# A decoder step on one core: the first stage in a new order, and the normalisation's root as a power on GpSimd

## The chip, the cores and the metric

The kernel runs on one core of one Trainium2 chip. The metric is the device time of the whole program in microseconds (us): the median of three runs. One more execution was taken by the hardware profiler. Its span (first to last instruction) and the rows of its trace are what this document argues from. The engines are TensorE (PE in the rows, PEld for its weight loads), VectorE (DVE), ScalarE (ACT), GpSimd (POOL) and SyncE (SP), which here only issues transfers. They run side by side and meet at semaphores.

## What is computed

One inference step of a decoder with two layers, for a prompt of 256 tokens and 8 sample streams of 4 tokens. The kernel holds all T = 288 tokens as columns of a transposed activation `xT` (128 partitions x 8 chunks x 288). Layer 0 mixes tokens by a diagonal complex state space (S5) with a gated linear unit (GLU), layer 1 by three groups of dilated attention. Each is followed by a PEER channel mixer with 16384 single-neuron experts. Every sub-layer normalises its input and shifts and scales it by vectors made from a condition `c`:

```
def rms_norm(x, gain=None):
    y = x32 * lax.rsqrt(jnp.mean(x32 * x32, axis=-1, keepdims=True) + EPS)
def adaln_params(c, w, b):
    return jnp.split(jax.nn.silu(c) @ w + b, 6, axis=-1)
def modulate(x, gain, shift, scale):
    return rms_norm(x, gain) * (1.0 + scale[:, None, :]) + shift[:, None, :]
def s5_mixer(h, h0, ...):
    a_bar = jnp.exp(lam * dt)
    b_bar = ((a_bar - 1.0) / lam)[..., None] * lax.complex(b_re, b_im)
    bu = jnp.einsum('bsgp,gnp->bsgn', u, b_bar)
    _, states = lax.associative_scan(_linear_recurrence_combine, (a, bu), axis=1)
    y = jnp.real(jnp.einsum('bsgn,gpn->bsgp', states, c_mat)) + d_skip * u
    z = y @ w_glu
    out = z[..., :D] * jax.nn.sigmoid(z[..., D:])
```

There are four such normalisations, q = 0 to 3: ahead of S5, of PEER 0, of attention and of PEER 1.

## The kernel before, in words

All large weights come through one stream of 680 tiles of 128 x 1024 fp32 (512 KB each) into a ring of four slots. SyncE issues the load of tile n as soon as TensorE has finished tile n - 4 (`tile_done`). The first 48 tiles are the adaLN weights of layer 0 (`ada0(k)`: `ada_tile`, 4 matrix products on 9 columns, line 1000 of the profile). They form six blocks of eight. ScalarE copies a finished block's rows out (`ada_row`, line 366, four instructions), and TensorE turns them into columns (`ada_turn`, line 1010, eight products) at the fourth tile of a later block. S5's normalised input needs blocks 0 and 1, the GLU's residual block 2, and PEER the rest.

The first stage, up to the GLU's first product (line 1161), works in a written order, with no planner:

- VectorE computes the powers of the transition (`times_a`, lines 1572 to 1576) up to `s5_w`, squares `xT` (`square_x`, line 1522), and reduces three small tables.
- `chunk_weights(q)` on TensorE (line 1049) spreads these powers over four PSUM banks, for q = 0 and 1. `chunk_products(q)` on VectorE (lines 1606 to 1613) multiplies them with the input matrix: four products that read PSUM and two sums. `spread_rows(q)` on ScalarE (line 643) puts the result into `ws`.
- For each of 8 chunks c, `turn_weights(c)` (line 1063) transposes `ws` into two PSUM banks, ScalarE copies both banks out in one instruction (line 665), and `token_weights(c)` (line 1075) multiplies them with the output matrix. They stand at k = 22 to 30 of the ada tiles, one chunk to a tile.
- Meanwhile VectorE fills the tables of cosines and sines by doubling (`while n < 64`, lines 1647 to 1653).
- `mean_square(0)` (line 1021) stands at k = 16. ScalarE takes the square root (`root_mean`, line 626), and VectorE's `modulate(0)` takes the reciprocal (line 1688), multiplies, scales and shifts (lines 1698 to 1707).
- The S5 loop over 8 chunks begins after ada tile 37 (`ADA0 = 38`). In it `s5_in(c)` (TensorE, line 1112) makes the scan's input; `rot_in(c)`, `scan(c)`, `out_weights(c+1)` and `y_low(c-1)` (VectorE, lines 1726 to 1777) rotate, scan, rotate back and prepare the next weights; `expand(c)` (ScalarE, line 684) and `s5_out(c)` (TensorE, lines 1128 and 1135) give the output; and `y_high(c)` copies it. Two ada tiles stand in each of the first five rounds.
- `high(act, GLU)` and `high(act, GLU + 1)`, line 372, split the first two GLU tiles in the rounds c = 5 and 6; GpSimd subtracts (line 2008) as soon as each is there.

The normalisations q = 1 to 3 have the same chain, with ScalarE squaring (line 618) and `mean_square(q)`, `root_mean(q)`, `modulate(q)` in a row. There TensorE has no other work until `modulate` is through its first half.

Of the kernel before, what the change touches and what calls it, by code (L numbers as in the profile page):

```python
# [5 lines left out]
P = 128  # L6
# [59 lines left out]
ADA0 = 38  # L66
# [22 lines left out]
def build(nc, I, O):  # L89
    ctx = ExitStack()  # L90
    with ctx:
# [37 lines left out]
        eps_c = sb("eps_c", 1)  # L129
        idx_t = sb("idx", 3 * T)  # L130
# [14 lines left out]
        class Region:  # L145
# [129 lines left out]
            "ada_row ada_turned ada_done us_norm sq_ready ms_ready std_ready h_ready s5_trig s5_thr s5_w s5_sel s5_we s5_m s5_st s5_pw s5_fill s5_dec s5_bu s5_rot s5_tr s5_tc s5_tm s5_tt s5_td s5_gc s5_cc s5_gz "  # L275
# [315 lines left out]
        def _(act):  # L591
# [55 lines left out]

            ada_row(act, 0, 0, 4)
# [4 lines left out]
            spread_rows(0)  # L653
# [4 lines left out]
            ada_row(act, 0, 1, 6)  # L658
# [14 lines left out]
            ada_row(act, 0, 3, 6)  # L673
# [20 lines left out]
            for c in range(NC):  # L694
                if c + 1 < NC:
                    expand(c + 1)
                y_high(c)
# [293 lines left out]
        def _(pe):  # L991
# [43 lines left out]
            def ada0(k):  # L1035
                nb, c = k // NC, k % NC
                if c == 0 and nb >= 2:
                    pe.wait_ge(S["ada_row"], nb if nb == 5 else nb - 1)
                ada_tile(0, k, 6 if nb in (1, 3) else 4)
# [13 lines left out]
            def turn_weights(c):  # L1053

                if c:
                    pe.wait_ge(S["s5_tc"], c)
                else:
                    pe.wait_ge(S["s5_m"], 2)
                    pe.wait_ge(S["s5_st"], 1)
                if c == 4:  # L1060
                    pe.wait_ge(S["s5_st"], 2)
# [1127 lines left out]
```

## Time and profile before

| what | value |
|---|---|
| median of 3 runs | 2479.38 us (2478.89, 2479.38, 2485.56) |
| the profiled execution | 2476.21 us, span 2474.3 us |
| PE / PEld busy | 96% / 89% of the span |
| DVE / ACT / POOL busy | 56% / 40% / 24% |
| mean granted TensorE clock | 0.974 of full |
| first stage | 0 to 179.67 us |
| read from HBM | 394.58 MB, 163 GB/s over the span |

Shares over the whole span say little about one stage: TensorE's 96% comes from the long PEER and GLU stretches. A stage's limit is read from the engine that has no gap in it, and from what ended the idle time of the others. A row of the timeline gives start, duration, engine, line, operation, output and inputs, the number of instructions merged into it, and in brackets the idle time before it with what ended it. Rows on PE overlap a little, since a matrix product's modelled end lies past the start of the next; the distance between two starts is the better measure.

### The profile page before, as it was taken

What the parts mean: (1) busy time and instruction counts of PE and PEld (TensorE: products, weight loads), DVE (VectorE), ACT (ScalarE), POOL (GpSimd) and SP (SyncE); (2) the same over time, 40 slices, a digit from 0 to 9 for tenths busy, and PEclk for the clock granted to TensorE, in tenths of its full rate; (3) what the DMA queues carried; (4) which work ended last, traced back from release to release, by engine and by line L of the source; (5) the groups of instructions that cost most, each with busy time, mean ns of one, the idle gap of its engine ahead of it and who ended that gap; (6) DMA issues with size and microseconds to landing.
All of it is one profiled execution on the core that took longest, in us unless ns stands there. A gap on an engine that the chain in (4) does not pass through costs nothing.

```text
span 2474.3 us, 51841 instructions
## 1 busy us (share of the span) xinstructions
PE 2365.4 (96%) x19526; PEld 2191.8 (89%) x19526; DVE 1380.4 (56%) x3302; ACT 988.0 (40%) x1669; POOL 601.2 (24%) x445
## 2 busy tenths in 40 slices
PE   6888999999999999999889977999999999999999
PEld 2578898999999999999888455899999999999999
DVE  5684269477888433333434132269788995333334
ACT  3334344444333444444443132444444444444443
POOL 1015456300000222222253000467300002222222
PEclk8889999999999999999989988999999999999999
DMA  6614456554544454555553663445433334554544
GB/s 242 205 67 141 153 163 212 192 175 171 179 168 140 148 186 163 168 162 169 181 183 114 240 254 130 142 151 165 149 128 127 127 127 144 181 169 161 168 162 146
DMA packets 114874, 405.50 MB, mean 164 GB/s; under 512 B 13275, under 2 KB 13403, under 8 KB 113723
## 3 DMA queue, kind: packets, MB, share of 16 engines
q1 hardware_dynamic: 111048, 388.68, 47.1%
q10 hardware_dynamic: 3699, 15.08, 1.5%
q8 instruction: 85, 1.39, 0.2%
q14 instruction: 42, 0.34, 0.0%
HBM read 394.58 MB, written 9.14 MB: 163 GB/s over the span
## 4 chain that ended last, share of the span: by engine, by line
PE 82%; issue 9%; POOL 4%; DMA 2%; ACT 2%; DVE 2%; ACTq 0%; SPq 0%; POOLq 0%; DVEq 0%
PE ps L1328 11%; PE ps L1332 11%; PE ps L1336 11%; PE ps L1191 10%; PE ps L1192 10%; PE ps L1195 10%; PE ps L1263 5%; POOL ring_lo L2001 2%; PE ps L1031 2%; PE ps L872 2%; DMA ring<-in_stream 1%; PE ps L1000 1%; POOL ring_lo L2008 1%; PE ps L758 1%; PE ps L751 1%
## 5 line engine op out<-in xcount | busy, mean ns | idle before, releaser
L372 ACT ACTIVATE wt_hi<-ring 128x1024 fp32r<-128x1024 f32 x552 | 580.4, 1051 | 575.7 <-PE ps L1195 400.4
L1953 DVE TENSOR_TENSOR ring_lo<-ring,wt_hi 128x1024 fp32r<-128x1024 f32 x256 | 315.4, 1232 | 494.8 <-ACT wt_hi L372 494.8
L1191 PE MATMUL ps<-split,wt_hi 128*128 128x288 f32 x2048 | 571.7, 305 | 3.2 <-ACT big L423 2.0
L1192 PE MATMUL ps<-split,wt_hi 128*128 128x288 f32 x2048 | 558.5, 297 | 0.0
L2027 POOL TENSOR_TENSOR split<-big,split 128x288 fp32r<-128x288 f32 x256 | 209.7, 819 | 1246.0 <-ACT split L473 648.7
L1191 PEld LDWEIGHTS ps<-split,wt_hi 128*128 128x128 f32 x2048 | 385.9, 188 | 11.7 <-issue 5.1
L1192 PEld LDWEIGHTS ps<-split,wt_hi 128*128 128x128 f32 x2048 | 386.1, 189 | 0.3
L1328 PE MATMUL ps<-split,wt_hi 128*128 128x288 f32 x2016 | 308.9, 295 | 5.7 <-DVE ada L1672 3.2
L1195 PE MATMUL ps<-split,ring_lo 128*128 128x288 f32 x2048 | 313.4, 295 | 0.4 <-POOL ring_lo L2001 0.4
L1332 PE MATMUL ps<-split,wt_hi 128*128 128x288 f32 x2016 | 309.0, 295 | 0.0
L1336 PE MATMUL ps<-split,ring_lo 128*128 128x288 f32 x2016 | 308.0, 294 | 0.0
L467 ACT ACTIVATE split<-big 128x288 fp32r (+1 forms) x252 | 112.0, 444 | 455.6 <-PE ps L1336 455.6
L2001 POOL TENSOR_TENSOR ring_lo<-ring,wt_hi 128x1024 fp32r<-128x1024 f32 x104 | 251.9, 2423 | 159.3 <-ACT wt_hi L372 159.1
L1195 PEld LDWEIGHTS ps<-split,ring_lo 128*128 128x128 f32 x2048 | 288.8, 189 | 0.7 <-POOL ring_lo L2001 0.6
L1328 PEld LDWEIGHTS ps<-split,wt_hi 128*128 128x128 f32 x2016 | 281.6, 188 | 6.1 <-issue 3.4
L1332 PEld LDWEIGHTS ps<-split,wt_hi 128*128 128x128 f32 x2016 | 281.9, 188 | 0.1
L1336 PEld LDWEIGHTS ps<-split,ring_lo 128*128 128x128 f32 x2016 | 281.1, 188 | 0.0
L1903 DVE TENSOR_TENSOR ring_lo<-ring,wt_hi 128x1024 fp32r<-128x1024 f32 x148 | 180.6, 1220 | 60.3 <-ACT wt_hi L372 60.1
L1913 DVE TENSOR_SCALAR xT<-consts,idx 128x128 f32<-128x128 f32 x576 | 198.4, 344 | 0.0
L1912 DVE TENSOR_SCALAR xT<-consts,idx 128x128 f32<-128x128 f32 x576 | 163.1, 283 | 0.0
L1263 PE MATMUL ps<-xT 128*128 128x128 f32 x1152 | 155.0, 277 | 0.0
L1263 PEld LDWEIGHTS ps<-xT 128*128 128x128 f32 x1152 | 141.7, 191 | 12.9 <-issue 9.5
(314 smaller groups left out, 2302.0 us busy)
## 6 DMA issues: line engine op xcount, KB each, us to landing
ring<-in_stream SPq DMA_DIRECT2D x680, 512.0 KB, 3.4
big<-in_kc SPq DMA_DIRECT2D x8, 1792.0 KB, 11.8
big<-in_vc SPq DMA_DIRECT2D x14, 1024.0 KB, 6.9
out_qk<-big ACTq DMA_DIRECT2D x1, 3456.0 KB
x_spill<-xT ACTq DMA_DIRECT2D x2, 1152.0 KB, 5.0
big<-x_spill ACTq DMA_DIRECT2D x2, 1152.0 KB, 6.3
out_v<-big ACTq DMA_DIRECT2D x1, 1536.0 KB
xT<-in_xT SPq DMA_DIRECT2D x1, 1152.0 KB, 10.8
```

Source lines behind the costliest of these rows:

```text
L372: nc.scalar.activation(wt_hi[:, n % 2 if b is None else b], ring[:, n % RING], ACT.Copy).then_inc(S["hi_ready"], 1)
L1191: mm(out, w, h_hi[:, c], start=(c == 0), stop=False)
L1192: mm(out, w, h_lo[:, c], start=False, stop=False)
L1195: ins = mm(out, ring_lo[:, slot, c * 128:(c + 1) * 128], h_hi[:, c], start=False, stop=(c == NC - 1))
L1263: ins = mm(ps[:, s % 2, 128 * t:128 * t + 128], oh[:, 0, s % 2, t, :], oh[:, 1, s % 2, t, :], start=True, stop=True)
L1328: mm(ps[:, c, 0:T], wt_hi[:, s % 2, c * 128:(c + 1) * 128], w_hi[:, s % 2], start=(first and s == 0), stop=False, skip_group_check=True)
L1332: mm(ps[:, c, 0:T], wt_hi[:, s % 2, c * 128:(c + 1) * 128], w_lo[:, s % 2], start=False, stop=False, skip_group_check=True)
L1336: ins = mm(ps[:, c, 0:T], ring_lo[:, s, c * 128:(c + 1) * 128], w_hi[:, s % 2], start=False, stop=False, skip_group_check=True)
L1913: ins = TS(oh[:, 1, q % 2, t], iota, idx[:, 1, n:n + 1], idx[:, 2, n:n + 1], ALU.is_equal, ALU.mult)
L1953: TT(ring_lo[:, s], ring[:, s], wt_hi[:, s % 2].bitcast(F32), ALU.subtract)\
L2001: TT(ring_lo[:, slot], ring[:, slot], wt_hi[:, s % 2].bitcast(F32), ALU.subtract)\
L2027: TT(w_lo[:, s % 2], W[:, bass.ds(4 * i + s, 1), :].rearrange("p a t -> p (a t)"), w_hi[:, s % 2].bitcast(F32), ALU.subtract).then_inc(S[" ...
```

## The change

The reciprocal of the root goes to GpSimd: ScalarE only forms mean + EPS (`Identity`), and GpSimd raises it to the power -0.5, from a column `power` filled once. This holds for all four q. Ahead of S5 the squares are ScalarE's. `ADA0` goes from 38 to 24, with 24 ada tiles left for the S5 loop, two or three a round, and the last `ada_turn` after `s5_out(7)`. The steps between move up, the copies of turned weights are halved, VectorE does small tables between the two `chunk_products`, and the second GLU tile is split a round later.

```
-ADA0 = 38
+ADA0 = 24
...
-                nc.scalar.activation(rstd if q else rstd0, ps[:, bank, 0:T], ACT.Sqrt, bias=eps_c[:, :], scale=1.0 / D)\
-                   .then_inc(S["std_ready"], 1)
+                nc.scalar.activation(rstd if q else rstd0, ps[:, bank, 0:T], ACT.Identity, bias=eps_c[:, :], scale=1.0 / D)\
+                   .then_inc(S["us_norm"], 1)
...
+            act.wait_ge(S["in_setup"], 16 * 4)
+            for m in (slice(0, 4), slice(4, 8)):
+                nc.scalar.activation(hT[:, m], xT[:, m], ACT.Square).then_inc(S["sq_ready"], 1)
             ada_row(act, 0, 0, 4)
...
             for c in range(NC):
-                act.wait_ge(S["s5_tr"], c + 1)
                 if c >= 2:
                     act.wait_ge(S["s5_tm"], c - 1)
-                nc.scalar.activation(wst[c % 2], ps[:, 0:2, :].rearrange("p b n -> p (b n)"), ACT.Copy).then_inc(S["s5_tc"], 1)
-                if c == 2:
-                    ada_row(act, 0, 2, 4)
+                for h in range(2):
+                    act.wait_ge(S["s5_tr"], 2 * c + h + 1)
+                    nc.scalar.activation(wst[c % 2][:, 512 * h:512 * h + 512], ps[:, h, :], ACT.Copy).then_inc(S["s5_tc"], 1)
+                if c == 1:
+                    ada_row(act, 0, 1, 6)
...
                 y_high(c)
-                if c == 0:
-                    ada_row(act, 0, 4, 4)
-                if c == 5:
-                    ada_row(act, 0, 5, 4)
-                    high(act, GLU)
-                if c == 6:
-                    high(act, GLU + 1)
+                if c in (1, 4):
+                    ada_row(act, 0, 3 + c // 4, 4)
+                if c >= 6:
+                    high(act, GLU + c - 6)
...
-                pe.wait_ge(S["s5_m"], q) if q else pe.wait_ge(S["s5_w"], 1)
+                pe.wait_ge(S["s5_mr"], q) if q else pe.wait_ge(S["s5_w"], 1)
...
-                if k == 5:
+                if k == 4:
                     pe.wait_ge(S["s5_sel"], 1)
                     chunk_weights(0)
+                if k == 9:
+                    chunk_weights(1)
                 if k == 11:
                     pe.wait_ge(S["in_k"], 16)
-                if k == 12:
-                    chunk_weights(1)
-                if k == 16:
                     mean_square(0)
-                if 22 <= k <= 30:
-                    if k > 22:
-                        token_weights(k - 23)
-                    if k < 30:
-                        turn_weights(k - 22)
+                if 14 <= k <= 22:
+                    if k < 22:
+                        turn_weights(k - 14)
+                    if k > 14:
+                        token_weights(k - 15)
                 ada0(k)
...
+            ada_at = (24, 27, 30, 32, 35, 38, 40, 43, 46, 48)
+            for c in range(NC):
+                s5_in(c)
                 if c:
                     s5_out(c - 1)
-                for k in range(ADA0 + 2 * c, min(48, ADA0 + 2 * c + 2)):
+                for k in range(ada_at[c], ada_at[c + 1]):
                     ada0(k)
-                if c == 7:
-                    ada_turn(0, 5, 7)
+            for k in range(46, 48):
+                ada0(k)
+            s5_out(NC - 1)
+            ada_turn(0, 5, 7)
...
-            v.wait_ge(S["in_setup"], 16 * 4)
-            square_x(0, hT)
...
+            chunk_products(0)
+            v.wait_ge(S["s5_m"], 1)
+            own.settle()
+            for n in (1, 2, 4):
+                turns(n)
+            chunk_products(1)
...
+            for n in (8, 16, 32):
+                turns(n)
...
-                own(nc.vector.reciprocal(r, r))
-                own.settle()
...
+            def root_mean(q):
+
+                pool.wait_ge(S["us_norm"], q + 1)
+                own.settle()
+                r = rstd if q else rstd0
+                TT(r, r, power[:, 0:1].broadcast_to([P, T]), ALU.pow).then_inc(S["std_ready"], 1)
```

On TensorE, at the program's start, before the change (1000: ada tiles, 4 instructions each; 1049: `chunk_weights`; 1010: `ada_turn`; 1021: `mean_square`):

```order
L1000 MATMUL ps<-ring,ccol 9x256 x20
L1049 MATMUL ps<-big 128x512 x4
L1000 MATMUL ps<-ring,ccol 9x256 x28
L1010 MATMUL ps<-consts,gtmp 128x9 x8
L1049 MATMUL ps<-big 128x512 x4
L1000 MATMUL ps<-ring,ccol 9x256 x16
L1021 MATMUL ps<-scratch,consts 128x288 x8
```

And after it (1003, 1052, 1013, 1024 are the same four; 1066 is `turn_weights`):

```order
L1003 MATMUL ps<-ring,ccol 9x256 x16
L1052 MATMUL ps<-big 128x512 x4
L1003 MATMUL ps<-ring,ccol 9x256 x20
L1052 MATMUL ps<-big 128x512 x4
L1003 MATMUL ps<-ring,ccol 9x256 x8
L1024 MATMUL ps<-scratch,consts 128x288 x8
L1003 MATMUL ps<-ring,ccol 9x256 x4
L1013 MATMUL ps<-consts,gtmp 128x9 x8
L1003 MATMUL ps<-ring,ccol 9x256 x8
L1066 MATMUL ps<-consts,big 128x128 x8
```

The second `chunk_weights` stands behind 9 ada tiles in place of 12 and an `ada_turn`, and the first transposes behind 14 tiles in place of 22.

On TensorE, from the last `token_weights` (1075) to the second `s5_in` (1112), before:

```order
L1075 MATMUL ps<-big 32x32 x32
L1000 MATMUL ps<-ring,ccol 9x256 x24
L1010 MATMUL ps<-consts,gtmp 128x9 x8
L1000 MATMUL ps<-ring,ccol 9x256 x8
L1112 MATMUL ps<-scratch,big 128x72 x32
L1000 MATMUL ps<-ring,ccol 9x256 x8
L1112 MATMUL ps<-scratch,big 128x72 x32
```

And after (1078 and 1114 are those two):

```order
L1078 MATMUL ps<-big 32x32 x32
L1003 MATMUL ps<-ring,ccol 9x256 x8
L1114 MATMUL ps<-scratch,big 128x72 x32
L1003 MATMUL ps<-ring,ccol 9x256 x12
L1114 MATMUL ps<-scratch,big 128x72 x32
```

Two tiles are left between the last turned weights and the loop, in place of eight and an `ada_turn`.

On TensorE, the end of the stage after the change, from the last round's third ada tile (1130 and 1137 are `s5_out(7)`, 1165 the GLU):

```order
L1003 MATMUL ps<-ring,ccol 9x256 x16
L1130 MATMUL ps<-scratch,big 32x288 x4
L1130 MATMUL ps<-scratch,big 32x72x3 x4
L1130 MATMUL ps<-scratch,big 32x72x2 x4
L1130 MATMUL ps<-scratch,big 32x72 x4
L1137 MATMUL ps<-big 32x72 x64
L1013 MATMUL ps<-consts,gtmp 128x9 x8
L1165 MATMUL ps<-split,wt_hi 128x288 x8
```

Before the change that last `ada_turn` stood ahead of `s5_out(7)`, and no ada tile stood in the last three rounds.

## Rows read from the trace of the kernel before

**Rows 1.** Table by stretch: PE, PEld, DVE, ACT, POOL busy, granted clock, DMA share, GB/s.
```profile
37.00:53.00 16.00, 15.40 (x65) 7.48 (x66) 6.48 (x24) 4.77 (x4) 0.00 (x0) 0.50 0.41 151
95.00:116.00 21.00, 20.05 (x292) 14.02 (x296) 8.72 (x19) 2.16 (x3) 0.00 (x0) 0.53 0.60 211
116.00:170.00 54.00, 49.36 (x1548) 39.68 (x1536) 51.83 (x113) 21.07 (x31) 2.53 (x1) 0.94 0.24 81
```
**Rows 2.** Timeline of DVE, the S5 loop.
```profile
107.07 1.42 DVE L1726 TENSOR_TENSOR big<-big,ps 128x576 f32<-128x576 f32 x2 [14.12 <-PE ps L1112]
108.53 0.46 DVE L1732 TENSOR_TENSOR big<-big 128x288 f32<-128x288 f32 x1
...
155.03 1.43 DVE L1767 TENSOR_TENSOR big<-big 128x256 f32<-128x256 f32 x4
...
163.21 3.63 DVE L1767 TENSOR_TENSOR big<-big 128x256 f32<-128x256 f32 x4
```
**Rows 3.** Timeline of PE, the same stage.
```profile
21.65 7.19 PE L1049 MATMUL ps<-big 64*128 64x512 f32 x8
28.77 3.60 PE L1000 MATMUL ps<-ring,ccol 128*9 128x256 f32 x32
33.41 0.62 PE L1000 MATMUL ps<-ring,ccol 128*9 128x256 f32 x8 [1.04 <-DMA ring<-in_stream]
...
74.35 1.09 PE L1063 MATMUL ps<-consts,big 128*128 128x128 f32 x8
...
76.56 0.76 PE L1075 MATMUL ps<-big 128*32 128x32 f32 x64 [0.56 <-ACT big L665]
77.25 1.09 PE L1063 MATMUL ps<-consts,big 128*128 128x128 f32 x8
...
97.96 3.58 PE L1010 MATMUL ps<-consts,gtmp 128*128 128x9 f32 x16
...
103.30 3.70 PE L1112 MATMUL ps<-scratch,big 32*128 32x72 f32 x64
...
175.67 4.07 PE L1135 MATMUL ps<-big 128*32 128x72 f32 x128 [5.75 <-DVE big L1757]
179.67 1.33 PE L1161 MATMUL ps<-split,wt_hi 128*128 128x288 f32 x8
```
**Rows 4.** Timeline of DVE ahead of the loop.
```profile
17.09 0.22 DVE L1576 TENSOR_TENSOR big<-big 128x64 f32<-128x64 f32 x1
...
49.38 1.23 DVE L1606 TENSOR_TENSOR big<-ps,big 128x1024 f32<-128x1024 f32 x1 [9.24 <-PE ps L1049]
...
76.42 0.49 DVE L1659 COPY big<-big 128x256 f32<-128x256 f32 x2
...
85.78 0.29 DVE L1707 TENSOR_TENSOR scratch<-scratch,ada 128x128 f32<-128x128 f32 x1
```
**Rows 5.** The root at q = 1, timeline of all engines.
```profile
232.01 4.15 PE L1021 MATMUL ps<-big,consts 128*128 128x288 f32 x16 [0.88 <-ACT big L618]
...
236.24 1.28 ACT L626 ACT_TABLE_LOAD   x1 [1.96 <-PE ps L1021]
...
238.06 1.95 DVE L1688 RECIPROCAL gtmp<-gtmp 128x288 f32<-128x288 f32 x1 [5.10 <-ACT gtmp L626]
240.05 1.36 DVE L1695 TENSOR_TENSOR big<-xT,gtmp 128x1152 f32<-128x1152 f32 x1
```
**Rows 6.** The same at q = 2 and q = 3.
```profile
1226.83 4.09 PE L1021 MATMUL ps<-big,consts 128*128 128x288 f32 x16
...
1233.85 1.36 DVE L1695 TENSOR_TENSOR big<-xT,gtmp 128x1152 f32<-128x1152 f32 x1
...
1530.28 4.15 PE L1021 MATMUL ps<-big,consts 128*128 128x288 f32 x16 [1.85 <-ACT big L618]
...
1536.98 1.36 DVE L1695 TENSOR_TENSOR big<-xT,gtmp 128x1152 f32<-128x1152 f32 x1
```
**Rows 7.** The page's groups: GpSimd's nearest operation in shape.
```profile
L2027 POOL TENSOR_TENSOR split<-big,split 128x288 fp32r<-128x288 f32 x256 | 209.7, 819 | 1246.0 <-ACT split L473 648.7
```

More of the change, by code:

```diff
@@ L129, in build @@
         eps_c = sb("eps_c", 1)
+        power = sb("power", 1)
         idx_t = sb("idx", 3 * T)
@@ L1053, in turn_weights @@
             def turn_weights(c):
[L1055 to L1061, printed above, removed]
-                for n in range(8):
-                    ins = nc.tensor.transpose(ps[:, n // 4, 128 * (n % 4):128 * (n % 4) + 128], ws[:, c, n // 2, n % 2, :], ident)
-                ins.then_inc(S["s5_tr"], 1)
+                if c == 0:
+                    pe.wait_ge(S["s5_mr"], 2)
+                if c % 4 == 0:
+                    pe.wait_ge(S["s5_st"], 1 + c // 4)
+                for h in range(2):
+                    if c:
+                        pe.wait_ge(S["s5_tc"], 2 * c + h - 1)
+                    for n in range(4):
+                        ins = nc.tensor.transpose(ps[:, h, 128 * n:128 * n + 128], ws[:, c, 2 * h + n // 2, n % 2, :], ident)
+                    ins.then_inc(S["s5_tr"], 1)
             def token_weights(c):
-                pe.wait_ge(S["s5_tc"], c + 1)
+                pe.wait_ge(S["s5_tc"], 2 * c + 2)
                 if c == 0:
@@ L1137, in s5_out @@
                 ins.then_inc(S["s5_ymm"], 1)
-            for c in range(NC + 1):
-                if c < NC:
-                    s5_in(c)
+            ada_at = (24, 27, 30, 32, 35, 38, 40, 43, 46, 48)
+            for c in range(NC):
+                s5_in(c)
                 if c:
                     s5_out(c - 1)
-                for k in range(ADA0 + 2 * c, min(48, ADA0 + 2 * c + 2)):
+                for k in range(ada_at[c], ada_at[c + 1]):
                     ada0(k)
-                if c == 7:
-                    ada_turn(0, 5, 7)
+            for k in range(46, 48):
+                ada0(k)
+            s5_out(NC - 1)
+            ada_turn(0, 5, 7)
             def glu(i, first):
@@ L1518, in _ @@
             own(nc.vector.memset(eps_c[:, :], EPS))
-            def square_x(q, dst):
-                for m in (slice(0, 4), slice(4, 8)):
-                    TT(dst[:, m], xT[:, m], xT[:, m], ALU.mult).then_inc(S["sq_ready"], 1)
             own.settle()
@@ L1608, in chunk_products @@
                 own(TT(mt[2], w[:, :, :, 0], im, ALU.mult))
-                own(TT(mt[3], w[:, :, :, 1], re, ALU.mult))
+                TT(mt[3], w[:, :, :, 1], re, ALU.mult).then_inc(S["s5_mr"], 1)
+                v.wait_ge(S["s5_mr"], q + 1)
                 own.settle()
@@ L1613, in chunk_products @@
                 TT(m[:, :, :, 1], mt[2], mt[3], ALU.add).then_inc(S["s5_m"], 1)
-            own.settle()
-            chunk_products(0)
             def square_e():
@@ L1638, in _, with turns @@
                 own.settle()
-            chunk_products(1)
-            own(TT(dt_t.rearrange("p (c m) -> p c m", c=NC), dg.unsqueeze(1).broadcast_to([P, NC, 32]),
-                   dskip.unsqueeze(2).broadcast_to([P, NC, 32]), ALU.mult))
-            v.wait_ge(S["s5_m"], 2)
-            n = 1
-            while n < 64:
+            def turns(n):
                 s1, s2 = (x[:, 0:PAIRS * n].rearrange("p (k t) -> p k t", k=PAIRS) for x in (s1_t, s2_t))
@@ L1656, in _ @@
                 own.settle()
-                n *= 2
+            chunk_products(0)
[4 more added lines that the diff above has]
+            chunk_products(1)
+            v.wait_ge(S["in_setup"], 16 * 4)
+            own(TT(dt_t.rearrange("p (c m) -> p c m", c=NC), dg.unsqueeze(1).broadcast_to([P, NC, 32]),
+                   dskip.unsqueeze(2).broadcast_to([P, NC, 32]), ALU.mult))
+            v.wait_ge(S["s5_m"], 2)
+            own.settle()
+            for n in (8, 16, 32):
+                turns(n)
             for tab in (tcos, tsin):
@@ L1687, in modulate @@
                 r = rstd if q else rstd0
-                own(nc.vector.reciprocal(r, r))
-                own.settle()
                 h = modsq if q else hT
@@ L1974, in _ @@
             TT, TS, CP = nc.gpsimd.tensor_tensor, nc.gpsimd.tensor_scalar, nc.gpsimd.tensor_copy
+            own(nc.gpsimd.memset(power[:, :], -0.5))
+            own.settle()
             nc.gpsimd.memset(lam_t[64:128].rearrange("p (q n) -> p q n", q=3)[:, :, 0:64], 1.0).then_inc(S["g_zero"], 1)
@@ L2032, in _ @@
             pool.wait_ge(S["tile_done"], VT[0] + 128)
+            root_mean(2)
             own(nc.gpsimd.memset(qz_t, 0.0))
```

18 lines of the change are left out of this document (11 added, 7 removed).

## The prediction

> **What bounds the kernel now.** I read the page first (engine shares, the 40 slices), then a table by stretch, then the timelines of VectorE and TensorE over the first 180 us, and last the four places where the root is taken. The span's shares mislead here: from 180 us on TensorE is full in nearly all slices and the change touches nothing there but three roots. The first stage ends when the GLU's first product starts, at 179.67 [rows 3], and has two parts with different limits.
>
> Up to 107 us VectorE is the one that waits. Its S5 loop starts at 107.07 after 14.12 us of idle time that TensorE's `s5_in` ended [rows 2]; this first `s5_in` starts only at 103.30 [rows 3], behind ada tile 37. So what counts is how soon TensorE reaches it. From 107 on VectorE is the limit: 51.83 us busy of the 54 from 116 to 170, while TensorE shows 49.36 [rows 1]. At 163.21 four products of `out_weights` take 3.63 us, where the same four take 1.43 a round earlier [rows 2]; GpSimd subtracts a GLU tile at that time, as it does once more in the round after. So a collision costs 2.2, and the eight rounds from 107.07 to 175.67 are 8.6 each with the two, 8.0 without. The last `s5_out` starts at 175.67, as soon as VectorE's scan is through, and the GLU 4.0 later [rows 3].
>
> **Part 1, TensorE up to the loop.** I lay the new order out from durations in rows. The clock was 0.50 of full from 37 to 53 us [rows 1], which is 1.2 GHz of 2.4; tiles from 28.77 go at the same pace (0.9 each, 3.60 for four), so I take the low level up to 50 us.
> - `chunk_weights(0)` stands at k = 4 and needs only the powers, done at 17.3 [rows 4]. It takes 7.1 (21.65 to 28.77 [rows 3]), to 24.4. Before, it waited for the fifth tile, to 21.65.
> - Tiles 4 to 7: 4 x 0.9, to 28.0. Tile 8 is asked for when tile 4 is done, 25.3. Before, tile 9 was asked for at 29.7 (tile 5 done) and used at 33.41 [rows 3], so 3.7 later: 29.0, done 29.9.
> - `chunk_weights(1)`: it needs only that VectorE's four products have read the banks, 4 x 1.2 [rows 4] after 24.4, at 29.3. So it starts at 29.9, to 37.0.
> - Tiles 9 and 10: 1.8, to 38.8. `mean_square(0)`, which took 4.15 at q = 1 [rows 5], 4.5 here, to 43.3. Tile 11 and the first `ada_turn`, 0.9 + 3.6 [rows 3], to 47.8. Tiles 12 and 13, to 49.6.
> - The turned weights: a round of transposes, tile and `token_weights` took 2.90 (74.35 to 77.25), 0.56 of it a wait for ScalarE's copy [rows 3]. Halved copies let the second half of the transposes run beside the first copy, so I take 2.35. First transposes 1.0, eight rounds 18.8, an `ada_turn` at the full clock 1.9, tile 23 and the last copy 1.0: to 72.3. If the half copies save nothing, 4.4 more.
> - `s5_in(0)` at 72.5 instead of 103.30. It then took 3.70 at the low clock; 3 is taken, so VectorE's loop starts at 75.5 instead of 107.07, 31.6 earlier.
>
> VectorE can keep that. From the second `chunk_products` to the end of the tables it was 27.5 (49.38 to 76.91 [rows 4]); from 37.0 that is 64.5 at the latest, and some 5 earlier as the three smallest tables now come ahead. It then waits for block 1's `ada_turn` at k = 19, about 65. From the tables to the end of `modulate` it was 9.2 (76.91 to 86.07 [rows 4]) with the reciprocal of 1.95 [rows 5], so 7.2 now, to about 72, and a little work on the turned weights behind it. It is ready shortly before 75.5. The squares (ScalarE now) and the root are done by 50, under this wait, so `modulate(0)` loses its reciprocal for nothing.
>
> **Part 2, the loop.** It was 68.6 (107.07 to 175.67). The second GLU tile is split a round later, behind VectorE's last scan, so one collision of 2.2 goes: 66.4, to 141.9. The 24 ada tiles in it, 2 or 3 a round at 0.5 to 0.9, are meant to lie in TensorE's free time: the scan's input for the next round is wanted some 8 us after the last one. Fourteen more tiles and one more `ada_turn` are 9 us at full clock against 4.6 us idle from 116 to 170 plus the 5.75 idle ahead of 175.67. The transfers fit: 24 tiles are 12.6 MB, 190 GB/s over 66 us, and the rows show 211 GB/s from 95 to 116 and only 81 after [rows 1]. Then `s5_out(7)` as before, 4.0, to 145.9, and after it the last `ada_turn`, once beside other work and now in front of the GLU: 1.9 to 3.6, I take 2.5. The GLU starts at 148.4 instead of 179.67: 31.3 saved.
>
> **Part 3, the roots at q = 1 to 3.** TensorE is idle there, so every microsecond counts. From the end of `mean_square` to VectorE's first product it was 236.16 to 240.05, 3.89 [rows 5]; 1230.92 to 1233.85, 2.93; 1534.43 to 1536.98, 2.55 [rows 6]; together 9.4. The table load of 1.28 is exposed at q = 1 only, the reciprocal of 1.95 at all. After the change each is 0.65 (ScalarE's pass 0.5, three handoffs) plus P, the power on GpSimd, 128x288. Saved: 7.4 - 3P.
>
> No row shows a power. Below, P cannot be less than GpSimd's subtraction of the same shape, 0.82 [rows 7]. VectorE's reciprocal is 4.25 times its plain product of that shape (1.95 against 0.46 [rows 5, 2]); the same ratio on GpSimd gives 3.5. A power as three such steps (logarithm, product, exponential) gives 10.4, my upper bound. I take 3.5, the one that is scaled from a measured hard function: 3.1 us lost. The ends are 4.9 gained and 23.8 lost. ScalarE's new table load ahead of attention's first root comes in front of its wait, as at q = 3, and is hidden, at worst 1.3.
>
> The row for GpSimd's plain work is 0.82 us for 288 elements, and it bears on price. The Trainium skill (GPSIMD Engine Reference, 3.1 Elementwise, side-by-side cycle accounting) says that this engine runs a software loop per element, about 2.6 cycles with two inputs and some 12 where it branches on data. By the first figure P would be 0.6, which the row of 0.82 contradicts slightly; by the second 288 x 12 cycles at 1.2 GHz are 2.9 us, an estimate, and the sum would be 1.3 lost instead of 3.1.
>
> **Sum.** -31.3 + 3.1 = -28.2. The profiled execution took 2476.21, so it would be 2448. The median of the runs shown is 3.2 higher, and the time asked is a median: 2479.4 - 28.2 = 2451.
>
> **The rivals.**
> 1. The power is cheap, P about 1. Same first stage, 4.4 gained at the roots: 2444. For it: GpSimd's subtraction takes under 3 ns an element [rows 7]. Against: VectorE's reciprocal shows that a non-linear function isn't priced like a sum.
> 2. The loop becomes TensorE's. If the clock falls to 1.2 GHz inside the loop, a round is 3.6 (`s5_in`, 3.70 in rows 3), about 2.6 and 2.9 for `s5_out`, and 3 tiles of 0.95: 12.0 against 8.0. Half the rounds so: 16 lost, 2467; all of them: 32 lost, 2483. For it: the clock was 0.53 from 95 to 116, just when the loop began behind waits for tiles. Against: 0.94 from 116 to 170 [rows 1], and TensorE gets more work in the loop, not less.
> 3. The power is slow at every root, P about 9.5: 18 more than my sum, 2469. The mechanism is a routine that isn't at hand when it is called, between long stretches of other operations, 6 us on top of 3.5, near the upper bound above. Against: the 256 calls of GpSimd's subtraction, with 1246 us of waits between them, still average 0.82 [rows 7]. The Trainium skill (GPSIMD Engine Reference, 2.1 Instruction dispatch) says that the first call of a freshly loaded kernel costs some 6 us that no row names; whether a power is such a kernel, or is loaded more than once, it doesn't say.
> 4. Slower than before: the power alone, at q = 1 to 3 with TensorE standing. From P = 13.0 the three roots eat the whole first stage (31.3 + 7.4 = 38.7, a third each), from 15.5 the kernel is over 0.3% slower; at P = 20 it would be 2500. It needs P above my upper bound from the rows.
> 5. The early tiles do nothing, since VectorE's own chain is late: it would need 31 us of new wait there, and by part 1 it has its own work done about when TensorE has. Only a few us of this can come true, in my own range.
>
> **How the numbers follow.** A measurement of this kernel can tell about 0.3%, 7.4 us, from no change. My forecast (P 2.5 to 6, loop on VectorE): 0.46, 2445 to 2460. Rival 1: 0.20. Rival 2: 0.13, of which 0.02 within 0.3% and 0.01 slower. Rival 3: 0.13. Rival 4: 0.05, of which 0.01 within. Rival 5 in full: 0.03, as no change or slower. So faster 0.92, same 0.04, slower 0.04. The range for 8 in 10 takes in rivals 1 and about half of 2 and 3: 2438 to 2468. The likeliest is 2451.
>
> **What would show it.** In the new profile: `chunk_weights(0)` at 17.3 and the second at about 30; first transposes at 50; `s5_in(0)` near 72, VectorE's first rotation near 75 with hardly any idle time ahead that TensorE ends; eight rounds of about 8 with one slow group; the GLU at 148 with an `ada_turn` just ahead; no table load at the four roots; and a power on GpSimd of 3.5 us, with 0.65 + 3.5 from mean square to product at each root. I am wrong if VectorE waits for `s5_in` inside the loop, if the transposes start after 60, or if the power's row is far from 3.5.

## The result: 5.3% slower, and the profile after

| | before | after |
|---|---|---|
| median of the runs beside each other | 2480.69 us (4 runs) | 2612.47 us (4 runs, 2606.72 to 2616.38) |
| ratio | | 1.0526, 95% interval 1.0498 to 1.0554 |
| profiled execution, time and span | 2476.21, 2474.3 | 2616.38, 2614.6 |
| GLU's first product starts | 179.67 | 185.74 |

I had forecast 2451, with 2438 to 2468 as the range. The cause that carries the loss stands in the page's groups of instructions. The columns are line, engine and operation, shapes, busy time and mean ns of one, idle time before it:

```profile
L2042 POOL TENSOR_TENSOR split<-big,split 128x288 fp32r<-128x288 f32 x256 | 210.1, 821 | 1244.7 <-ACT split L474 649.4
...
L1990 POOL TENSOR_TENSOR gtmp<-gtmp,power 128x288 f32<-128x288 f32 x3 | 138.7, 46219 | 183.8 <-ACT gtmp L627 183.8
```

The subtraction that I took as the lower bound costs what it did [rows 7]; the power beside it, of the same shape, takes 46.2 us, 56 times as long. Who waits for it, from VectorE's waits in the whole span (total us, times, longest):

```profile
DVE big L1699 <- POOL gtmp L1990: 147.2, 3, 50.1
```

And the root at q = 1, in the timeline of all engines (start, duration, line, idle time before it and its releaser); it answers to [rows 5]:

```profile
238.06 4.15 PE L1024 MATMUL ps<-big,consts 128*128 128x288 f32 x16 [0.88 <-ACT big L619]
...
242.30 0.50 ACT L627 ACTIVATE gtmp<-ps,eps_c 128x288 f32<-128x288 f32 x1 [1.97 <-PE ps L1024]
242.88 46.22 POOL L1990 TENSOR_TENSOR gtmp<-gtmp,power 128x288 f32<-128x288 f32 x1 [8.52 <-ACT gtmp L627]
289.14 1.36 DVE L1699 TENSOR_TENSOR big<-xT,gtmp 128x1152 f32<-128x1152 f32 x1 [50.12 <-POOL gtmp L1990]
```

From the end of the mean square (242.21) to VectorE's product it is 46.93, where it was 3.89. At q = 2 and 3 the power stands alone in the same way, at 1283.58 and 1631.05. Three times 46.9 against 9.4 before [rows 5, 6]: 131.4 lost. Nothing covers it: from 243 to 289 the table by stretch gives every engine but GpSimd 0.00 us of work, TensorE too.

The first stage got 6.1 us longer, though it was to be 31.3 shorter. The rows of the first root, on GpSimd and VectorE:

```profile
44.50 46.36 POOL L1990 TENSOR_TENSOR big<-big,power 128x288 f32<-128x288 f32 x1 [21.80 <-ACT big L627]
```
```profile
90.96 1.36 DVE L1702 TENSOR_TENSOR scratch<-xT,big 128x1152 f32<-128x1152 f32 x1 [26.50 <-POOL big L1990]
```

VectorE was ready at 64.46. The power had 20 us of cover there and overran it by 26.5. TensorE's row of the first `s5_in`, and a line of the table by stretch (width, then busy time of PE, PEld, DVE, ACT and POOL, granted clock, DMA share, GB/s):

```profile
17.87 7.16 PE L1052 MATMUL ps<-big 64*128 64x512 f32 x8 [3.19 <-DVE big L1576]
...
30.44 7.19 PE L1052 MATMUL ps<-big 64*128 64x512 f32 x8
...
39.38 4.50 PE L1024 MATMUL ps<-scratch,consts 128*128 128x288 f32 x16
...
47.23 1.09 PE L1066 MATMUL ps<-consts,big 128*128 128x128 f32 x8
...
95.91 2.42 PE L1114 MATMUL ps<-scratch,big 32*128 32x72 f32 x40 [26.43 <-DVE scratch L1711]
```
```profile
72.00:90.00 18.00, 0.00 (x0) 0.00 (x0) 0.00 (x0) 0.00 (x0) 18.00 (x1) 0.56 0.12 45
```

`chunk_weights` at 17.87 and 30.44, mean square at 39.38 and the first transposes at 47.23 are near where I had laid them (17.3, 29.9, 38.8, 50), the transposes 2.8 early. Then, in the 18 us of the table's line, every engine but GpSimd is idle.

From the first `s5_in` to the GLU it is 89.8 us; it was 76.4 (103.30 to 179.67 [rows 3]). So a second loss hides in the loop. Here are the rows on TensorE that have "issue" as the releaser (idle time that ends by nothing the profile shows), and VectorE's wait behind the longest of them:

```profile
109.73 0.64 PE L1137 MATMUL ps<-big 128*32 128x72 f32 x27 [0.25 <-issue]
119.89 0.77 PE L1137 MATMUL ps<-big 128*32 128x72 f32 x36 [0.85 <-issue]
128.87 0.58 PE L1137 MATMUL ps<-big 128*32 128x72 f32 x24 [1.75 <-issue]
140.22 0.81 PE L1137 MATMUL ps<-big 128*32 128x72 f32 x17 [3.83 <-issue]
...
162.86 0.38 PE L1137 MATMUL ps<-big 128*32 128x72 f32 x9 [0.79 <-issue]
...
172.61 0.25 PE L1137 MATMUL ps<-big 128*32 128x72 f32 x2 [2.12 <-issue]
```
```profile
150.92 1.42 DVE L1730 TENSOR_TENSOR big<-big,ps 128x576 f32<-128x576 f32 x2 [8.96 <-PE ps L1114]
```

The theory from here: (a) a power on GpSimd costs about 46 us whenever it is called, and explains the whole loss; (b) the new order by itself makes the kernel faster, but by about half of what I forecast, and the other half goes in the loop. Rivals: to (a), a cold routine (my rival 3), or a price that hangs on the values; to (b), that the new order itself loses, or that the loop is as long as before whatever stands in it.

### The profile page after: what moved, and what is told of

Same layout as the page of the kernel before. It is cut to its first block, busy times and chain, and to the rows that moved or that the text cites. A ratio compares the mean times of both kernels' runs of the same rounds, so it can differ in the third digit from the quotient of the medians.

```text
span 2614.6 us, 51855 instructions
## 1 busy us (share of the span) xinstructions
PE 2358.3 (90%) x19526; PEld 2187.3 (84%) x19526; DVE 1374.5 (53%) x3296; ACT 987.6 (38%) x1676; POOL 786.4 (30%) x450
## 4 chain that ended last, share of the span: by engine, by line
PE 82%; POOL 9%; issue 4%; DVE 2%; ACT 1%; DMA 1%; ACTq 0%; POOLq 0%; SPq 0%; DVEq 0%
PE ps L1332 10%; PE ps L1336 10%; PE ps L1340 10%; PE ps L1195 9%; PE ps L1196 9%; PE ps L1199 9%; POOL gtmp L1990 5%; PE ps L1267 5%; POOL ring_lo L2015 2%; PE ps L1034 2%; POOL big L1990 2%; PE ps L875 2%; PE ps L1003 1%; PE ps L761 1%; PE ps L754 1%
## 5 line engine op out<-in xcount | busy, mean ns | idle before, releaser
L373 ACT ACTIVATE wt_hi<-ring 128x1024 fp32r<-128x1024 f32 x552 | 580.4, 1052 | 588.2 <-PE ps L1199 410.7
L1917 DVE TENSOR_SCALAR xT<-consts,idx 128x128 f32<-128x128 f32 x576 | 197.2, 342 | 0.0
L1990 POOL TENSOR_TENSOR gtmp<-gtmp,power 128x288 f32<-128x288 f32 x3 | 138.7, 46219 | 183.8 <-ACT gtmp L627 183.8
L1034 PE MATMUL ps<-big,ring 128*128 128x288 f32 x320 | 82.9, 424 | 101.8 <-DVE big L1711 99.7
L1034 PEld LDWEIGHTS ps<-big,ring 128*128 128x128 f32 x320 | 63.4, 199 | 121.1 <-DVE big L1711 100.6
```

Of the source, the lines that this page charges most:

```text
L373: nc.scalar.activation(wt_hi[:, n % 2 if b is None else b], ring[:, n % RING], ACT.Copy).then_inc(S["hi_ready"], 1)
L1034: ins = mm(out, ring[:, s, off + c * 128:off + (c + 1) * 128], rhs[:, c, :], start=(c == 0), stop=(c == chunks - 1))
L1990: TT(r, r, power[:, 0:1].broadcast_to([P, T]), ALU.pow).then_inc(S["std_ready"], 1)
```

## The experiments

**The two halves of the change, each alone.** order_only is the changed kernel with the old roots:

```diff
-                nc.scalar.activation(rstd if q else rstd0, ps[:, bank, 0:T], ACT.Identity, bias=eps_c[:, :], scale=1.0 / D)\
-                   .then_inc(S["us_norm"], 1)
+                nc.scalar.activation(rstd if q else rstd0, ps[:, bank, 0:T], ACT.Sqrt, bias=eps_c[:, :], scale=1.0 / D)\
+                   .then_inc(S["std_ready"], 1)
...
+                own(nc.vector.reciprocal(r, r))
+                own.settle()
...
-            root_mean(0)
...
-                root_mean(2 * l + 1)
...
-            root_mean(2)
```

> The new order with the old root at all four places (root on ScalarE, reciprocal on VectorE). Theory 1 (the two halves of the change are separate: the power costs 46 us at each of the three bare roots and 26.5 at the first, and the order alone gains): the S5 loop starts near 75 us as predicted; if the loop then takes the 84.6 us that it took after the change (101.1 to 185.7), the GLU starts near 160 and the time is about 2460; if it takes the predicted 73, GLU near 148 and 2450. Rival (the new order itself loses, by TensorE's work in the loop): GLU at 180 or later, 2480 or more.

Measured: 2458.94 us (2452.91 to 2460.59) against 2477.61, ratio 0.9913 (0.9891 to 0.9936), with the GLU at 163.54. The new order is a gain of 18.7 us, as the theory's 2460 has it; the GLU is 3.5 later than its 160. power_only is the kernel before with `root_mean` on GpSimd at all four roots:

> The old order with the power on GpSimd at all four roots. Theory 1: three bare roots at 46.2 + 0.65 us each in place of 9.4 together, +131; and at the first root ada tile 27 waits for it, from 81.7 to about 104, +22: about 2634. Rival (the power is slow only in the new order, through contention with VectorE or TensorE there): near 2490.

Measured: 2633.76 (2630.93 to 2635.33), ratio 1.0627 (1.0608 to 1.0647), the 2634 that was expected. It loses 156.2. The sum of both, 137.5, is 5.7 over the 131.8 that the whole change lost. Of this, 1.4 stand at the GLU, which the first power moves by 23.6 in the old order (179.67 to 203.28) and by 22.2 in the new; the rest isn't explained. The powers are the loss and the order isn't.

**Where the power's loss lies.** root0_only is the changed kernel with the power at q = 0 alone (`ACT.Sqrt if q else ACT.Identity`, `if q: reciprocal`).

> The changed kernel with the power at the first root (q = 0) alone; the three later roots are a root on ScalarE and a reciprocal on VectorE again. It splits the loss of 153.5 us between the first root, ahead of the loop, and the three at which TensorE stands. Theory (the first power keeps VectorE from modulate for 26.5 us and moves the loop as a whole, 95.91 against order_only's 72.39 for the first s5_in): the GLU at 185 to 187 instead of 163.5, and 22 to 24 us over order_only, 2481 to 2483. Rival (a late loop runs against fewer transfers and takes part of it back, since the ring is full when it starts): the GLU before 182, under 2478.

Measured, one run: 2482.88, so 23.9 over order_only, with the GLU at 184.02, 1 us ahead of the theory's band and 2 behind the rival's. The first power costs about 24, and the other three 2612.5 - 2482.9 = 129.6, which is the 131.4 of the rows above within 2. (The kernel before was itself 2.5 slower beside this run than beside order_only, so the 24 may be 21; at the GLU it is 20.5.)

**What the power is paid for.** prices: two calls of half the columns at q = 1, 64 partitions at q = 2 (the other 64 keep the mean square), a quarter of the columns at q = 3 (the rest keeps it). Parts of the power are left out, so the kernel's values are wrong; only the durations are read.

```diff
...
+                e = power[:, 0:1]
+                if q == 1:
+                    own(TT(r[:, 0:144], r[:, 0:144], e.broadcast_to([P, 144]), ALU.pow))
+                    TT(r[:, 144:T], r[:, 144:T], e.broadcast_to([P, 144]), ALU.pow).then_inc(S["std_ready"], 1)
+                elif q == 2:
+                    TT(r[0:64], r[0:64], e[0:64].broadcast_to([64, T]), ALU.pow).then_inc(S["std_ready"], 1)
+                elif q == 3:
+                    TT(r[:, 0:72], r[:, 0:72], e.broadcast_to([P, 72]), ALU.pow).then_inc(S["std_ready"], 1)
...
```

> The kernel after the change with the power cut in other shapes; at two roots part of it is left out. Root 1: two instructions of 128x144. Root 2: partitions 0 to 63 alone (the others get no power). Root 3: columns 0 to 71 alone. If the time is a price per column: 23 us each, 46 us, 11.6 us. If it is a fixed cost of the call (a routine brought in): all near 46, so root 1 takes 92. If all 128 partitions share one unit: 23 us at root 2.

```profile
232.06 23.30 POOL L1992 TENSOR_TENSOR gtmp<-gtmp,power 128x144 f32<-128x144 f32 x1 [8.52 <-ACT gtmp L627]
255.33 23.30 POOL L1993 TENSOR_TENSOR gtmp<-gtmp,power 128x144 f32<-128x144 f32 x1
...
1274.04 46.21 POOL L1995 TENSOR_TENSOR gtmp<-gtmp,power 64x288 f32<-64x288 f32 x1 [9.98 <-ACT gtmp L627]
...
1618.06 11.84 POOL L1997 TENSOR_TENSOR gtmp<-gtmp,power 128x72 f32<-128x72 f32 x1 [161.88 <-ACT gtmp L627]
```

prices2: 8 partitions at q = 1, an exponent of 2 (a tile `two` in place of `power`) at q = 2, 16 partitions at q = 3; again the rest keeps the mean square.

> The same, with other cuts. Root 1: partitions 0 to 7 alone; root 3: partitions 0 to 15 alone (the others get no power). Root 2: the exponent is 2 in place of -0.5, so the values are other ones. If the 16 partitions that one GpSimd core serves go one after another, 23 us at root 1 and 46 at root 3; if they go in step, 46 at both. If the routine is a general one, the exponent changes nothing: 46 at root 2.

```profile
239.47 46.21 POOL L1993 TENSOR_TENSOR gtmp<-gtmp,power 8x288 f32<-8x288 f32 x1 [8.54 <-ACT gtmp L628]
...
1279.43 46.22 POOL L1995 TENSOR_TENSOR gtmp<-gtmp,two 128x288 f32<-128x288 f32 x1 [9.98 <-ACT gtmp L628]
...
1627.92 46.20 POOL L1997 TENSOR_TENSOR gtmp<-gtmp,power 16x288 f32<-16x288 f32 x1 [164.53 <-ACT gtmp L628]
```

The durations are a line through three shapes: 11.84, 23.30 and 46.22 us for 72, 144 and 288 columns, so 0.159 us a column and 0.4 fixed. From 8 to 128 partitions nothing changes, nor with the exponent (46.22 for 2), which settles the rival of the values as far as two exponents and four roots can. The second call of a pair, right behind the first, takes as long as the first, and the line leaves 0.4 for anything fixed: a cold routine is excluded, in any size that would matter here.

**What the loop pays for.** order_only's loop shows the gaps of after's but the first of 0.25, with the same numbers of matmuls behind them (36, 24, 17, 9, 2) and lengths of 0.72, 1.75, 3.10, 0.93 and 2.11, 8.6 us in all. Rows of TensorE, then of VectorE, then the table by stretch:

```profile
72.39 3.71 PE L1114 MATMUL ps<-scratch,big 32*128 32x72 f32 x64 [3.72 <-DVE scratch L1713]
...
117.60 0.50 PE L1137 MATMUL ps<-big 128*32 128x72 f32 x17 [3.10 <-issue]
...
118.47 3.58 PE L1013 MATMUL ps<-consts,gtmp 128*128 128x9 f32 x16
...
150.54 0.25 PE L1137 MATMUL ps<-big 128*32 128x72 f32 x2 [2.11 <-issue]
...
153.50 3.60 PE L1003 MATMUL ps<-ring,ccol 128*9 128x256 f32 x32
157.04 2.62 PE L1130 MATMUL ps<-scratch,big 32*32 32x288 f32 x32
...
163.54 1.30 PE L1165 MATMUL ps<-split,wt_hi 128*128 128x288 f32 x8
```
```profile
127.58 1.42 DVE L1732 TENSOR_TENSOR big<-big,ps 128x576 f32<-128x576 f32 x2 [8.11 <-PE ps L1114]
```
```profile
105.00:120.00 15.00, 10.14 (x300) 7.90 (x289) 13.66 (x31) 3.80 (x5) 0.00 (x0) 0.95 0.37 113
120.00:135.00 15.00, 15.00 (x297) 11.59 (x301) 7.22 (x16) 2.49 (x6) 0.00 (x0) 0.60 0.32 106
```

TensorE is busy 10.14 of 15 us and stands 3.10 in one piece. Behind that gap, from 120 to 135, its granted clock is 0.60, so most of this stretch is at the lower level: an `ada_turn` takes 3.58 where one at full clock takes 1.95, and `s5_in` 3.71 where one at full clock takes 2.34. VectorE then waits 8.11. small_loads asks what the gaps hang on. It is order_only with 20 of the loop's 24 tiles loaded to 32 of 1024 columns, so most of their data is left out and the adaLN values are wrong:

```diff
-            with sp.Fori(1, upos(0, MIX0) // RING) as i:
+            for a, b, w in ((1, 7, 1024), (7, 12, 32), (12, upos(0, MIX0) // RING, 1024)):
...
-                    load(i, s, RING * i + s)
+                        sp.dma_start(ring[:, s, 0:w], stream[bass.ds(RING * i + s, 1)].rearrange("a p n -> (a p) n")[:, 0:w])\
+                          .then_inc(tile_in[s], 16)
```

> order_only with one change: the transfers of tiles 28 to 47 of the weight stream (the block 0 adaLN weights that are used around and in the S5 loop) move 32 of 1024 columns each, so most of that weight data is left out and the adaLN values of block 0 are not right. Nothing else moves. It asks where the new order's loop loses 15 us against my prediction. Theory A (the gaps of 1.75, 3.10 and 2.11 us that TensorE shows inside the loop with no releaser come from the weight transfers, which take the memory that TensorE's instructions are fetched through): the gaps shrink to 0.9 or less, the clock stays near 0.9 in the loop, VectorE loses its wait of 8 us for s5_in(5), and the GLU starts at about 150 to 155 instead of 163.5. Theory B (the gaps come with the work or with the instruction stream itself): the gaps stay within 0.5 us of what they were, and so does the GLU, at 160 to 164.

Measured, one run: 2447.51. The rows that answer to order_only's:

```profile
74.38 3.70 PE L1117 MATMUL ps<-scratch,big 32*128 32x72 f32 x64 [3.80 <-DVE scratch L1716]
...
130.22 0.38 PE L1140 MATMUL ps<-big 128*32 128x72 f32 x9 [1.47 <-issue]
...
138.65 0.25 PE L1140 MATMUL ps<-big 128*32 128x72 f32 x2 [0.81 <-issue]
...
150.16 1.31 PE L1168 MATMUL ps<-split,wt_hi 128*128 128x288 f32 x8
```
```profile
105.00:120.00 15.00, 14.14 (x405) 11.02 (x399) 14.59 (x35) 3.72 (x6) 0.00 (x0) 1.00 0.06 10
120.00:135.00 15.00, 13.22 (x456) 10.62 (x448) 14.59 (x33) 6.41 (x10) 0.00 (x0) 1.00 0.05 9
```

The gaps of 0.7, 1.75 and 3.10 are gone, the clock is 1.00, VectorE is busy 14.59 of each 15 us, and it is 75.8 from `s5_in(0)` to the GLU where order_only has 91.2. Theory A holds, except that one gap went the wrong way (0.93 to 1.47). So the loop's length hangs on the weight transfers, though no matmul in it waits for a weight. How much is theirs is less sure than one difference, 15.4, makes it look: kernels with order_only's loop take 88.0 to 91.2 in four profiles (the table below), so it is 12 to 15. And the GLU is only 13.4 earlier, since `s5_in(0)` comes 2.0 later here (74.38).

**Fourteen tiles ahead of the loop again.** tiles_first: `ADA0 = 38`, two tiles a round, and with them the copies of the rows of block 3 ahead of the loop and the last `ada_turn` ahead of `s5_out(7)`, as in the kernel before.

> order_only with one part undone: all of tiles 24 to 37 stand ahead of the loop again, as in the kernel before (with the new early places of chunk_weights, mean square and the turned weights kept), and two ada tiles a round in it. It asks what moving 14 tiles into the loop is worth. By my prediction (tiles in the loop are free) it must lose nearly all the time of these tiles: 14 tiles at 0.9 to 1.2 us, so s5_in(0) at 85 to 90 instead of 72.4, the GLU 13 to 15 later than my 148.4 but, since the loop has then its undisturbed 66 to 68, at about 155 to 160, which would be below order_only's 163.5: about 2452 to 2456. By the rival (the loop takes as long as before, 76 from first s5_in to GLU, whatever stands in it; the gain was all made ahead of it): GLU at 162 to 166, 2457 to 2462. If the tiles in the loop really pay as they stand: GLU over 168, over 2463.

Measured: 2469.69 (2465.81 to 2474.32), ratio 0.9964 (0.9950 to 0.9977); GLU at 173.51, the third outcome. My estimate of 0.9 to 1.2 us a tile was off: `s5_in(0)` starts at 96.45, 24 us later for 14 tiles, which are 7.3 MB and wait for the ring:

```profile
75.00:90.00 15.00, 10.89 (x84) 4.86 (x80) 3.69 (x10) 3.60 (x6) 0.87 (x2) 0.61 0.85 308
```

Its loop then takes 77.1, with 2.7 us of gaps in place of 8.6. So a tile costs 1.7 us ahead of the loop (24.1 for 14) and 0.8 to 1.0 in it (77.1 against 88.0 to 91.2); both prices hold a share of the two `ada_turn` that move with the tiles. That difference is why moving the tiles pays, not that the loop is free: it moves the GLU from 173.51 to 163.54. The other 6.2 us of the 16.1, from 179.67 to 173.51, come from the rest of the order.

**Half copies.** whole_copies puts ScalarE's copy of a round of turned weights back into one piece of 1024 columns.

> order_only with one part undone: ScalarE copies each round of turned weights in one piece of 1024 columns again, and TensorE's next transposes wait for the whole copy. It tests the term 2.90 - 2.35 a round of my part 1. Theory: the eight rounds from the first transposes take 8 x 0.55 = 4.4 us longer, and so does the first s5_in, at 75 to 77 instead of 72.4 (there VectorE's chain had 3.7 us of TensorE's idle time in front of it, so less than 4.4 can arrive). Rival (half copies save nothing, since ScalarE pays its fixed cost twice): same within 0.7 us.

Measured, one run: 2463.20, with `s5_in(0)` at 74.28, 1.9 later than in order_only: neither the theory's 75 to 77 nor the rival's 0.7. The rows of the turned weights on TensorE tell what it is. The first chunk's transposes stand at 42.02; these are those of the chunks 1, 3 and 4:

```profile
49.25 1.97 PE L1065 MATMUL ps<-consts,big 128*128 128x128 f32 x8 [5.59 <-ACT big L668]
...
56.16 1.09 PE L1065 MATMUL ps<-consts,big 128*128 128x128 f32 x8
...
58.52 1.06 PE L1065 MATMUL ps<-consts,big 128*128 128x128 f32 x8
```

At the full clock a round takes 2.36 with whole copies (56.16 to 58.52), and in order_only, with half copies, 2.20 to 2.32. On the length of a round the rival is right. The two rounds from 49.25 take 3.76 and 3.15: the granted clock is 0.58 from 49.2 to 56, after TensorE had stood 5.59 us for ScalarE's first copy. The same happened in small_loads, which has half copies: it stood 5.02, the clock was 0.64 behind it, and its `s5_in(0)` came at 74.38. So the 1.9 us aren't the copies'.

**Versions of the loop.** best is order_only with 26 tiles ahead of the loop, two tiles in place of five between the last `s5_in` and the last `s5_out` (the expectation below says none, but tiles 46 and 47 stand there), `ada_turn(0, 5, 7)` inside the last `s5_out`, and a dummy root that brings ScalarE's table in ahead of the wait at q = 1:

```diff
-ADA0 = 24
+ADA0 = 26
...
+            nc.scalar.activation(small[:, 0:1], eps_c[:, :], ACT.Sqrt, bias=eps_c[:, :])
...
+                if c == 7:
+                    ada_turn(0, 5, 7)
...
-            ada_at = (24, 27, 30, 32, 35, 38, 40, 43, 46, 48)
+            ada_at = (26, 29, 32, 35, 38, 40, 43, 46, 48)
```

> order_only with three changes to the loop and its end: two more tiles ahead of the loop (26), none between the last s5_in and the last s5_out, the last ada_turn split into the last s5_out so that it runs beside VectorE's last readout, and a dummy root on ScalarE right after the squares' and sums' last use so that the table of the root at q = 1 is loaded ahead of its wait (1.3 us). Theory (the last 10 us ahead of the GLU in order_only are TensorE at half clock with ada_turn and five tiles in front of s5_out(7)): the GLU at 152 to 158, and 2448 to 2453. Rival (TensorE falls behind by the gaps in rounds 3 to 6 in any case, and VectorE's wait of 8 us stays): GLU at 160 to 164, 2455 to 2459.

Measured: 2455.20 (2448.21 to 2467.82), ratio 0.9907 (0.9883 to 0.9931). The GLU starts at 158.33, 5.2 earlier and between the two theories; the time lies in the rival's band, and the times can't tell the version from order_only. The table load is out of the way (ScalarE, all rows of the place):

```profile
213.59 1.28 ACT L726 ACT_TABLE_LOAD   x1
214.89 0.29 ACT L726 ACTIVATE small<-eps_c 128x1 f32<-128x1 f32 x1
215.55 0.50 ACT L627 ACTIVATE gtmp<-ps,eps_c 128x288 f32<-128x288 f32 x1 [0.37 <-PE ps L1023]
```

In order_only ScalarE waits 1.96 for the mean square's end and the load of 1.28 starts only then, at 220.08. tiles_between puts a round's tiles between `s5_in` and `s5_out`:

> The version called best with one change: the ada tiles of a round stand between s5_in and s5_out, where TensorE waits for VectorE's readout in the undisturbed rounds (1.28, 0.86 and 0.32 us in small_loads), instead of behind s5_out. Theory (TensorE's time in a round is short only by its gaps, and a tile in such a wait is free): no wait of VectorE for s5_in, GLU at 152 to 155, 2447 to 2451. Rival (the tiles' transfers still meet the same points of the instruction stream, and the gaps of 0.7 to 2.7 us only move): GLU at 157 to 161, 2453 to 2457.

Measured: 2458.21 (2456.01 to 2461.36), ratio 0.9916 (0.9897 to 0.9935), GLU at 158.72. The rival is right on the GLU, and the time is 1.2 over its band: the gaps now fall into `s5_in`, 4.3 us in six pieces.

The loop of all versions, from TensorE's rows (us):

| | tiles in the loop | "issue" gaps in it | s5_in(0) to GLU |
|---|---|---|---|
| before | 10 | 2.6 | 76.4 |
| tiles_first | 10 | 2.7 | 77.1 |
| small_loads | 24, without most of their data | 2.3 | 75.8 |
| tiles_between | 22 | 4.3 | 83.7 |
| best | 22 | 6.0 | 84.6 |
| whole_copies | 24 | 7.7 | 88.0 |
| root0_only | 24 | 7.8 | 88.4 |
| after | 24 | 9.6 | 89.8 |
| order_only | 24 | 8.6 | 91.2 |

The last four have the same loop and differ by 3.2, so a difference of 1 us, as between best and tiles_between, says nothing.

## Why the prediction was wrong

**Part 1 came out right in its time, partly by luck.** `s5_in(0)` was to start at 72.5, and without the powers it starts at 72.39. TensorE was ready at 68.67, 3.8 before my 72.5, and then stood 3.72 for VectorE's chain, a thing I had put the other way round by a hair. VectorE's chain was long for a reason that I hadn't in it. The end of the turned weights sets GpSimd free for a MEMSET, and this now meets `modulate(0)`. Rows of order_only, VectorE's and then GpSimd's:

```profile
67.28 4.64 DVE L1709 TENSOR_SCALAR scratch<-scratch,ada 128x256 f32<-128x256 f32 x4
...
73.76 1.37 DVE L1709 TENSOR_SCALAR scratch<-scratch,ada 128x256 f32<-128x256 f32 x4
```
```profile
67.87 3.59 POOL L2005 MEMSET big<- 128x4096 f32 x1 [45.39 <-PE ps L1078]
```

Four passes take 4.64 beside the MEMSET and 1.37 without it, 3.3 lost on the path. Without that, VectorE would have released `s5_in(0)` at about 69.0 (an estimate, 72.25 - 3.27), so the agreement within 0.1 us is an offset of two misses. VectorE's own loop was to start at 75.5 and starts at 77.60. The round of 2.35 us was right in size (2.2 to 2.4 in the rows) but not by the half copies: whole ones give the same. What remains of the edit is the order, `token_weights` of the round before now standing between the transposes and their use, beside the copy. That this is the cause was not tried by itself.

**Part 2 was mis-sized, and with it the first stage: 31.3 forecast, 16.1 measured** (179.67 to 163.54 in order_only). The step that failed is "The 24 ada tiles in it ... are meant to lie in TensorE's free time", with "The transfers fit". The loop was to be 75.9 from `s5_in(0)` to the GLU and took 91.2; with the transfers all but gone it takes 75.8. On the path, the 15.4 between these two runs are 10.4 in VectorE's rounds, 9.9 of it waits for `s5_in` (8.1 in the one round behind the gap of 3.10; such a wait was a sign of being wrong that I had named), and 4.9 at the end: in order_only TensorE reaches the last `s5_out` at 159.59, 8.3 after VectorE is through (151.33), in small_loads 3.3 after it (142.89 to 146.21). So at the end the tiles and the `ada_turn` in front of it aren't in free time even without their transfers, and that 75.8 meets 75.9 is partly luck: VectorE's loop started 5.2 behind `s5_in(0)` and not 3, and the last `s5_out` and `ada_turn` took 3.95 and not 6.5. I had asked whether the bytes fit (190 GB/s) and not what else they hold up. The lower clock in the loop is what rival 2 described; it stands in the rows behind the longest gap, a place that rival 2 didn't name. The collision of 2.2 is gone as forecast: from VectorE's first rotation at 100.22 to the last `s5_out` at 169.65 tiles_first takes 69.4, 3.8 of it waits for `s5_in`, so 65.6 against my 66.4. (A second such collision is left there, 3.38 at 165.12 where a round before has 1.43; order_only has neither.)

**Part 3 failed, and it alone turned the sign.** The step is "A power as three such steps (logarithm, product, exponential) gives 10.4, my upper bound"; "I take 3.5". P is 46.2. The formula around it was right: 0.65 + P forecast, 46.93 - 46.22 = 0.71 measured. With P = 46.22 in it, 7.4 - 3P gives -131.3, the 131.4 of the rows. Rival 4 had the mechanism and its point, slower than before from P = 13.0, and I gave it 0.05, since "It needs P above my upper bound from the rows". That bound wasn't one. It took the ratio of two VectorE rows over to GpSimd, where no row showed it, and multiplied by a count of steps that no row showed either. No row held a power, nor any GpSimd function but sums and copies: the honest upper end was open. Rival 4 also left out the first root: I had it "under this wait", which holds for P up to 20 (44.50 to 64.46); at 46.2 it moves the GLU by 22.2.

Rival 3's cold call is excluded: the first power takes 46.36 and the others 46.22, and the pair of halves 23.30 each. By the Trainium skill (GPSIMD Engine Reference, 3.1 Elementwise, side-by-side cycle accounting) I had estimated 2.9 us from some 12 cycles an element; the runs show 159 ns a column, which at the 1.2 GHz used there would be 190 cycles. The measurement decides.

The whole, from the rows: order -16.1 at the GLU, first power +22.2 (185.74 - 163.54), three powers +131.4, together +137.5; the two profiled executions differ by 140.2, and 2.7 stay unexplained. The split into order and first power leans on one profile of order_only, whose loop is the longest of its kind, so it is sure to about 3 us.

## What to carry to other kernels

An operation that no row shows has no upper bound from rows of other operations: measure it by itself before it goes onto a path on which TensorE stands, or write down an open end and the break-even beside it. When an instruction costs by the column and not by the partition, put the values across partitions (not tried here), or compute them elsewhere; here the root with ScalarE (0.50) and the reciprocal with VectorE (1.95), 2.5 us, were the cheap way. And work that fits into an engine's free time still brings its transfers along: ask what else travels with them, and compare the price of a tile in its old place (1.7 us) with that in its new one (0.8 to 1.0), not with zero. And when a chain moves, look at what its end sets free: here a MEMSET on GpSimd, which then cost VectorE 3.3 us.

## What the runs showed of the hardware

- A power as a two-input instruction on GpSimd takes 0.4 + 0.159 us a column (72 to 288 columns), alike for 8 to 128 partitions, exponents -0.5 and 2, first and later calls.
- TensorE has idle stretches that no semaphore ends. In the changed kernel, order_only, root0_only and whole_copies, which have the same loop, they stand at the same places of its instruction stream (36, 24, 17, 9 and 2 matmuls ahead of the same points), 0.4 to 3.8 us long. With the weight transfers cut (small_loads) three of the five are gone, one is shorter (0.81) and one is longer (1.47). The profile lists a queue of kind instruction among the DMA queues; in order_only it has one packet in the 5 us around the longest gap:

```profile
q1 hardware_dynamic: 181, 0.63, 32.0%
q8 instruction: 1, 0.02, 1.2%
```

  That TensorE waits there for its instructions, which wait behind the ring's transfers, fits the places and the effect of the transfers, but no row names it. Such packets come every 5 to 6 us, beside gaps and away from them (13 of this queue from 74 to 150 in order_only, 15 in small_loads), and one gap grew without the transfers. It stays an explanation that was argued.
- Four VectorE passes of 128x256 take 1.37 us alone and 4.64 beside a MEMSET of 128x4096 on GpSimd (order_only, small_loads); in the changed kernel, where they meet its last part, 2.87.
- A table load on ScalarE stands behind the wait of the pass that needs it, or ahead of it when a small pass with the same function comes first: 1.28 us either in the path or out of it.
